# Hybrid decoder step: overflow expert tiles with a prefetched input, residual rows kept in SBUF, router weights stationary

## The reference

```python
mixed = jnp.concatenate([a_out, b_out], axis=-1) @ w_out
x = layer_norm(DEEPNORM_ALPHA * x + gate1 * mixed, ln1_g, ln1_b)
h = x * (1 + scale2) + shift2
f = hier_moe(h, w_group_router, w_expert_router, w_gate, w_up, w_down)
x = layer_norm(DEEPNORM_ALPHA * x + gate2 * f, ln2_g, ln2_b)
```

## Time and profile before

| | us |
|---|---|
| median of 3 runs | 1577.37 (1575.47 to 1581.02) |
| the profiled execution | 1579.47 |
| its span, first to last instruction | 1577.6 |

### The profile page before, as it was taken

The page is one execution under the profiler, slowest core; times in us unless marked ns, Lnnn a source line. Parts: engine busy times, 40 slices in busy tenths (PEclk is TensorE's granted clock), DMA queues, the critical chain, the costliest instruction groups (busy, mean ns, idle before and its releaser), DMA issues. The chain is left out here.

```text
span 1577.6 us, 24986 instructions
## 1 busy us (share of the span) xinstructions
PE 1420.0 (90%) x9447; PEld 676.1 (43%) x9447; DVE 574.1 (36%) x1273; ACT 365.1 (23%) x809; POOL 323.3 (20%) x494
## 2 busy tenths in 40 slices
PE   5989988899999899996299999999999999999954
PEld 2644444444556544553244444444444444444421
DVE  1246999960355367436710111011101111111128
ACT  1334555311566421010011111111111111000014
POOL 0217444596100024321000000000000000000036
PEclk8999999999899999987599999999999999999977
DMA  8717222221121254312869999999999999999745
GB/s 330 288 32 256 67 65 82 72 76 60 36 78 33 81 151 161 130 58 98 325 241 379 389 405 399 408 409 404 399 409 407 403 399 407 401 395 389 303 158 185
DMA packets 98559, 385.29 MB, mean 244 GB/s; under 512 B 19808, under 2 KB 37280, under 8 KB 85181
## 3 DMA queue, kind: packets, MB, share of 16 engines
q1 hardware_dynamic: 75228, 327.54, 53.8%
q10 hardware_dynamic: 16384, 32.52, 6.1%
q0 software_dynamic: 6880, 24.38, 5.0%
HBM read 344.39 MB, written 40.00 MB: 244 GB/s over the span
## 5 line engine op out<-in xcount | busy, mean ns | idle before, releaser
L1854 PE MATMUL psum<-wgu,xgT 128*32 128x256 f32 (+1 forms) x3840 | 429.7, 454 | 10.7 <-DVE xgT L2026 9.3
L1854 PEld LDWEIGHTS psum<-wgu,xgT 128*32 128x32 f32 (+1 forms) x3840 | 173.1, 119 | 262.7 <-issue 203.4
L678 PE MATMUL psum<-w_sb,mixT 128*128 128x512 f32 x512 | 230.1, 603 | 13.6 <-ACT u L873 7.9
L1863 PE MATMUL psum<-wd,hidT 128*32 128x256 f32 (+1 forms) x1920 | 220.7, 454 | 0.0
L678 PEld LDWEIGHTS psum<-w_sb,mixT 128*128 128x128 f32 x512 | 95.9, 192 | 137.0 <-issue 112.1
L1905 POOL DMA_INDIRECT xg<-h_dram,tokens x32 | 29.5, 922 | 531.2 <-PE psum L1846 483.4
L1863 PEld LDWEIGHTS psum<-wd,hidT 128*32 128x32 f32 (+1 forms) x1920 | 79.9, 119 | 127.1 <-issue 100.9
L2032 DVE TENSOR_TENSOR hid<-silu,psum 128x256 f32<-128x256 f32 x40 | 16.9, 422 | 286.2 <-ACT silu L1973 286.2
L1434 PE MATMUL psum<-w_o,mixT 128*128 128x512 f32 x256 | 114.7, 608 | 1.1 <-PEq L1165 1.1
L980 DVE TENSOR_SCALAR_CACHE_REDUCE above<-bias,cand 128x384 int8<-128x384 f32 (+3 forms) x128 | 108.2, 846 | 4.5
L1973 ACT ACTIVATE silu<-psum 128x256 f32<-128x256 f32 x40 | 15.3, 383 | 348.1 <-PE psum L1854 348.1
(11 more groups left out here) (365 smaller groups left out, 1593.4 us busy)
## 6 DMA issues: line engine op xcount, KB each, us to landing
wgu<-in_w_gate_dram SPq DMA_DIRECT2D x40, 2048.0 KB, 17.1
wgu<-in_w_up_dram SPq DMA_DIRECT2D x40, 2048.0 KB, 22.0
wd<-in_w_down_dram SPq DMA_DIRECT2D x40, 2048.0 KB, 22.5
ada_b<-in_w_ada_dram ACTq DMA_DIRECT2D x16, 1024.0 KB, 5.0
ys_dram<-yy ACTq DMA_DIRECT2D x80, 128.0 KB, 8.5
ys_dram<-zero SPq DMA_DIRECT2D x22, 384.0 KB, 5.1
ada_a<-in_w_ada_dram SPq DMA_DIRECT2D x4, 2048.0 KB, 15.3
w_sb<-in_w_in_dram SPq DMA_DIRECT2D x4, 2048.0 KB, 10.2
```

The costliest lines, as they stand in the source:

```text
L678: last = nc.tensor.matmul(bank[2 + n % 2], mixT[:, k, t * P:(t + 1) * P], w_sb[:, k, n0:n0 + 512], start=(k == 0), stop=(k == DC - 1))
L1854: last = nc.tensor.matmul(out[m * j:m * j + m, 0:2 * w], xgT[:, b, k, first:first + m], wgu[:, b, :, k, w * j:w * j + w], start=(k == 0), ...
L1863: last = nc.tensor.matmul(out[m * j:m * j + m, 0:w], hT(k), wd[:, b, k, w * j:w * j + w], start=(k == 0), stop=(k == KD - 1))
```

## The change

There are three edits.

1. Overflow tiles run the code of main tiles. The last main tile and every overflow tile transpose the input of the next tile while they wait for their hidden values, and ACT and DVE copy one bank each. The input gathers run one tile further (one more column of the token list, which names row 0), so the last tile prefetches one input that nobody uses.
2. x1 is not stored to DRAM and read back. POOL (and DVE for the last tile) writes x1 of a prompt tile into that tile's columns of `mixT`, which nobody reads after the tile's projection. Only the 32 sample rows go through DRAM. `mixT` is kept to the end of the kernel in place of the array `x1`. In the last block the finished rows go to four rotating buffers `yo`, and DVE waits from the fifth tile on until the store from its buffer has landed.
3. The router weights are the stationary operand (36 columns to load) and `h2T` the moving one (up to 128 columns to stream). The result has the 36 logits in the partitions. ACT copies it to `lgT`, PE transposes it back (`turn_back`, one tile later in the list, for the last tile at once), and ACT copies that to `logit`.

The core of the diff:

```diff
-            x1_tile = [x1_dram[t * P:t * P + rows(t), :] for t in range(TA)]
+            back = slice(3 * P, 3 * P + NG + NE)
+            def wide(y):
+                return y.rearrange("p (c n) -> p c n", n=P)
+            def x1_of(t, r, b):
+                return mixT[:, :, t * P:(t + 1) * P] if t < TILES else wide(z[0:r, b, :])
...
-                        sp.wait_ge(d_x1, n + 1)
-                        sp.dma_start(x1_tile[t], z[0:r, n % 2, :]).then_inc(d_st[n % 2], 16)
+                        if t == TILES:
+                            sp.wait_ge(d_x1, n + 1)
+                            sp.dma_start(x1_dram, z[0:r, n % 2, :]).then_inc(d_sx, 16)
...
                         if n >= 1:
-                            pe.wait_ge(d_lge, n)
+                            pe.wait_ge(d_lte, n)
...
-                            last = nc.tensor.matmul(bank[6][0:r, 0:NG + NE], h2T[:, k, 0:r], rw[:, k, :], start=(k == 0), stop=(k == DC - 1))
+                            last = nc.tensor.matmul(bank[6][0:NG + NE, 0:r], rw[:, k, :], h2T[:, k, 0:r], start=(k == 0), stop=(k == DC - 1))
...
+                    def turn_back(n):
+                        r = rows(DT[n])
+                        pe.wait_ge(d_lge, n + 1)
+                        if n == 3:
+                            pe.wait_ge(c_trpe, 4)
+                        nc.tensor.transpose(bank[6][0:r, back], lgT[:, 0:r], c("ident", NG + NE)[:, 0:NG + NE]).then_inc(d_lt, 1)
...
+                        if n >= 2:
+                            turn_back(n - 2)
...
+                    turn_back(TA - 2)
                     logits(TA - 1)
+                    turn_back(TA - 1)
...
-                        nc.scalar.activation(logit[0:r, t, :], bank[6][0:r, 0:NG + NE], ACT.Copy).then_inc(d_lge, 1)
+                        nc.scalar.activation(lgT[:, 0:r], bank[6][0:NG + NE, 0:r], ACT.Copy).then_inc(d_lge, 1)
...
-                        g.tensor_tensor(z[0:r, b, :], z[0:r, b, :], vec["ln1_g"][0:r, :], ALU.mult).then_inc(d_pool, 1)
+                        g.tensor_tensor(x1t, wide(z[0:r, b, :]), wide(vec["ln1_g"][0:r, :]), ALU.mult).then_inc(d_pool, 1)
...
-                    for t in range(TILES):
-                        sp.dma_start(x1[:, t, :], x1_dram[t * P:(t + 1) * P, :]).then_inc(g_x[t % 4], 16)
...
-                    for e in range(NE):
+                    for e in range(NE + 1):
...
-                        if prefetch:
-                            pe.wait_ge(f_x[1 - b], 16 * (half + 1 + b))
-                            x_transposes(1 - b).then_inc(f_tx, 1)
+                        pe.wait_ge(f_x[1 - b], 16 * (half + 1 + b))
+                        x_transposes(1 - b).then_inc(f_tx, 1)
...
-                    extras(pe, n_extra, extra)
+                    steps(pe, expert)
+                    extras(pe, n_extra, expert)
...
                     def extra(e, b, half):
-                        x_whole(e, b)
                         hids(e)
+                        x_part(e + 1, 1 - b)
                         hidT(e)
...
-                        sp.dma_start(y_tile[t], x1[0:r, t, :]).then_inc(g_st[t % 4], 16)
+                        sp.dma_start(y_tile[t], yo[0:r, t % 4, :]).then_inc(g_st[t % 4], 16)
...
-                            v.scalar_tensor_tensor(out=x2, in0=x2, scalar=rstd[0:r2, (t - 2) % 3, :], in1=vec2["ln2_b"][0:r2, :],
+                            if t >= 6:
+                                dve.wait_ge(g_st[(t - 2) % 4], 16 * ((t - 2) // 4))
+                            v.scalar_tensor_tensor(out=wide(yo[0:r2, (t - 2) % 4, :]), in0=x2, scalar=rstd[0:r2, (t - 2) % 3, :], in1=wide(vec2["ln2_b"][0:r2, :]),
```

More of the change, by code:

```diff
@@ L1454, in _, with logit_rows, prob_parts @@
                             last.then_inc(d_mm, 1)
+                    turn_back(TA - 2)
                     logits(TA - 1)
+                    turn_back(TA - 1)
                 @block.scalar
                 def _(act):
+                    def logit_rows(n):
+                        r = rows(DT[n])
+                        act.wait_ge(d_lt, n + 1)
+                        nc.scalar.activation(logit[0:r, DT[n], :], bank[6][0:r, back], ACT.Copy).then_inc(d_lte, 1)
+                    def prob_parts(j):
+                        act.wait_ge(c_trp, j + 1)
+                        nc.scalar.activation(prT[:, j, :, 0:P], bank[7].rearrange("p (k n) -> p k n", k=NPG), ACT.Copy).then_inc(c_trpe, 1)
+                        nc.scalar.activation(pnT[:, j, 0:P], bank[6][0:NS, (1 + j) * P:(2 + j) * P], ACT.Copy).then_inc(c_trpe, 1)
                     for n, t in enumerate(DT):
                         r = rows(t)
+                        if n >= 1:
+                            logit_rows(n - 1)
+                        if n == 3:
+                            prob_parts(0)
                         for j in range(2):
@@ L1472, in _ @@
                                                      accum_out=st[:, j, 2:3]).then_inc(c_exp, 1)
[L1473 to L1477, removed]
+                        if n == 3:
+                            prob_parts(1)
                         if n == 4:
@@ L1604, in step_kernel @@
         g_gv = sem(keep, "g_gv")
-        x1 = sb(keep, "x1", [P, TILES + 1, D])
-        g_x = [sem(keep, f"g_x{i}") for i in range(4)]
+        x1_s = sb(keep, "x1_s", [NS, D])
+        g_x = sem(keep, "g_x")
         weights = keep.enter_context(ExitStack())
@@ L1775, in _ @@
                         pe.wait_ge(e_one, 2 * n + 2)
-                        last = nc.tensor.matmul(bank[4][:, 0:SLOTS], onepos[:, n, :], onetile[:, n, :], start=(n == 0), stop=(n == 2 * TA - 1))
+                        last = nc.tensor.matmul(bank[4][:, 0:SLOTS + 1], onepos[:, n, :], onetile[:, n, :], start=(n == 0), stop=(n == 2 * TA - 1))
                     last.then_inc(e_list, 1)
@@ L1906, in _ @@
                                                      in_offset=bass.IndirectOffsetOnAxis(ap=tokens[0:CAP, e:e + 1].bitcast(U32), axis=0)).then_inc(f_x[e % 2], 16)
-                    for i in range(MAXEXTRA):
-                        with pool.If(n_extra > i):
+                    for i in range(1, MAXEXTRA + 1):
+                        with pool.If(n_extra > i - 1):
                             pool.wait_ge(f_tx, NE + i - 1)
@@ L1993, in step @@
                         silus(e)
-                        if not (type(e) is int and e == NE - 1):
-                            x_part(e + 1, 1 - b)
+                        x_part(e + 1, 1 - b)
                         act.wait_ge(f_d1, e + 1)
@@ L2075, in step_kernel, with wide, x1_of @@
             dev = sb(ctx, "dev", [P, 2, D])
+            yo = sb(ctx, "yo", [P, 4, D])
             nmean = sb(ctx, "nmean", [P, 3, 1])
+            def wide(y):
+                return y.rearrange("p (c n) -> p c n", n=P)
+            def x1_of(t):
+                return mixT[:, :, t * P:(t + 1) * P] if t < TILES else wide(x1_s[:, :])
             rstd = sb(ctx, "rstd", [P, 3, 1])
```

76 lines of the change are left out of this document (39 added, 37 removed).

## The result

The changed kernel takes 1561.73 us (median of 5 runs, 1560.23 to 1564.74) against 1575.47 beside it (5 runs, 1574.45 to 1581.02): ratio 0.991, 95% interval 0.9889 to 0.9932. Its profiled execution took 1561.62 with a span of 1559.4; before it was 1579.47 and 1577.6. HBM writes fell from 40.00 to 35.81 MB. The forecast was 1564.1, the range 1560.5 to 1569.5.

What follows compares the result with a forecast made beforehand. PE was taken to set the experts' pace, with the DMAs beginning to set it late in the main tiles. The terms -14.7 + 0.3 + 0 + 1.1 = -13.3 us gave 1564.1 against the median of 1577.37; range 1560.5 to 1569.5.

Steps and rivals of the forecast that it cites:

- Overflow tiles, -14.7: Eight overflow tiles at the main tiles' pace, two intervals at 17.40 and six at 17.60 us: 14.7 us gained.
- 0.3 more at the end: After the last overflow tile's hidden product, transposes for an input nobody uses: +0.3 us.
- my lower bound of 12.3: Least gain forecast for the overflow tiles: two intervals at 17.40 and six at 18.0 us.
- DMAs at 393 GB/s: Rival: DMAs hold the overflow tiles at this rate, gain 12.3 in place of 14.7, time 1566.5 us; chance 0.08.
- Store loop: Overflow tiles' wait for the previous tile's stores: 16.4 us loop, costed at nothing; as rival up to 5 us, chance 0.04.
- x1 in SBUF, 0: Keeping x1 in SBUF removes stores and loads that nothing waited for, and strided access costs nothing: 0 us.
- Router, +1.1: Projection and router block: 0.6 us saved in groups, 0.9 added by transposes back, 0.8 at the end; +1.1 us.
- my bounds: Range for the router edit's effect on the projection and router block: -0.6 to +6.0 us.
- signs that I had named for being right: Overflow tiles 17.4 to 17.7 apart, no xgT wait, DMA 400 GB/s or more, last block 62 us, routing within 2.
- those for being wrong: PE waiting over 0.5 us a tile for up-weights, silu late behind store waits, DVE on x over 1.4, PE gaps.

Runs made afterwards that it cites:

- the part alone: The kernel before with only the overflow tiles changed to prefetch the next tile's transposes; 1562.57 us, ratio 0.9919.
- its variants with all weights: The changed kernel with store waits by tile parity (1561.24 us, ratio 0.9905), and that with empty overflow conditions nested (1561.93 us, ratio 0.9890).
- three kernels with the old router: The kernel before with overflow prefetch alone (1562.57 us), with the old router padded to 128 columns too (1557.72), and with resident x1 on top (1559.57).

## Why the prediction was right, and which of its steps failed

The time came out 2.4 us under the forecast and inside the range. Of this, 1.9 is the baseline, which stood at 1575.47 beside the changed kernel and not at 1577.37: the change gave -13.7 between medians, where I had said -13.3. That closeness is luck in good part. The sum has two failed terms that nearly cancel, the overflow tiles (3 us less than forecast) and the router block (3.5 us shorter in place of 1.1 longer).

- **Overflow tiles, -14.7: mis-sized.** The mechanism is right: no wait for xgT, the transposes where PE waited anyway, 0.3 more at the end. In the part alone the gain is 155.1 - 140.8 = 14.3, and my six tiles at 17.60 and two at 17.40 (140.4) were within 0.4 of it. In the whole change it is 11.7 in one profile, 11.5 in the other, under my lower bound of 12.3. The difference is mostly one weight load, late by about 2 us and not made up. In four profiles of the changed kernel and its variants with all weights, the tiles sum to 143.4, 143.7, 141.2 and 144.0, three times with an interval of 19.6 to 20.2; in three kernels with the old router to 140.8, 140.5 and 141.5 with none. Resident x1 alone doesn't bring it (the 141.5 has it, in one profile), nor does the new router in every execution (the 141.2 has it), and with three of four against none of three, chance isn't excluded. What delays the load stays open. The lower bound was built from a uniformly lower rate; the loss came as one event.
- **DMAs at 393 GB/s.** That the DMAs hold the new tiles above 17.40 is shown by the kernel without w_down loads. As to the rate, the overflow part alone moved 403 GB/s from 1363 to 1460 and took 17.60 a tile, against the rival's 18.0. In the whole change it was 397 GB/s, and the gain of 11.7 lies nearer to the rival's 12.3 than to my 14.7: on this stage the rival was the better guess. The figure of about 358 GB/s in the Trainium skill, page "DMA: Bandwidth & Descriptors", section "Where 436 GB/s comes from", doesn't bind here, with one core running: the changed kernel moves 404 GB/s over 88 us, as the one before did.
- **Store loop.** It cost nothing, as the step said, but the step had its size wrong. I had a loop of 16.4 us, under the tile's 17.4, so hardly a wait; the copies of ACT that waited for stores came up to 17.9 apart (1399.34 to 1417.26), and ACT waited up to 5.6. What saved the term is the slack ahead of the next silu, 3.0 us behind such a wait (I had about 2.4). With the wait the tiles take 17.60, without it 17.65.
- **x1 in SBUF, 0.** Right: 1.0011 [0.9996, 1.0026].
- **Router, +1.1: wrong in sign.** At equal clock it is +3.1, inside my bounds: 0.3 on average for each of the six steps with a transpose back (I had 0.13 for the transpose and nothing for the later start of what follows w_o), 0.9 for the tail (I had 0.8), and only 0.04 saved in each group, where 1.98 became 1.94 (I had 0.08). The failed step is one that wasn't taken: rows 2 showed a granted clock of 0.90 in a stretch in which PE was busy 89% of the time, and I read the shapes of its passes for their duration and never asked what the clock did behind them. That is 7.1 us, more than any of the terms I worked out for this part.

Without the clock the sum by measured parts would be -11.7 + 0.3 + 3.1 = -8.3; with it, -15.4; the rest of the span's 18.2, 2.8 us, lies in stages that vary so from execution to execution.

Of the signs that I had named for being right, two came: no wait of PE for xgT, and the last block no longer than before. Three didn't: four of the eight intervals lay above 17.7, the DMAs moved 397 GB/s there and not 400, and the routing started 4.0 us earlier. Of those for being wrong, ACT's copy to yy did wait for stores, with no late silu behind it, and PE waited for up-weights by 0.46 us a tile on average, just under the 0.5 that I had set.

## What to carry to other kernels

Read the granted clock of a block before you cost an edit in it: where PE is busy and the clock is below 1, look which group stands ahead of the slow one, and try that group with more streamed columns, even unused ones; here 92 unused columns a pass made the kernel 6.5 us faster. When a tile is brought down to the rate of its loads, look for single late loads too, and not only at the mean rate. A wait that the profile shows in full (24 us of it here) can cost nothing, as it did where the next silu waited for PE anyway: vary it alone before you mend it.

## What the hardware did that I had not expected

- With 36 streamed columns in the router's passes the granted clock dips between 640 and 720 us in all five profiles, while PE is busy; with 128, in none of nine. In the kernel before, the dip makes the group behind it 8.45 us long in place of 5.45.
- 14 empty conditions cost 2.5 us more than a nested form that skips them (19.95 and 17.41 us from the last hidden product to the gather), and the profile doesn't count them as busy time of any engine.
- The DMAs moved 404 GB/s over 88 us (1253 to 1341) and 400 over 453 us (800 to 1253) in the changed kernel, with one core running, in loads of 2 MB with gathers and small stores among them.
